# One head's queries first, the log table fetched early, the last pair one by one, and the delta rule's outputs ahead of the third chunk's sums

## The chip, the cores and the metric

The kernel runs on one core of one Trainium2 chip, in one launch. The metric is the device time of the launch in microseconds, the median of three executions: 3196.31 us before the change (3195.89, 3196.31, 3202.15).

## The reference

The input x has 512 tokens of width 1024. 16 meta tokens are put ahead of them, so a first block sees 528. Everything is float32.

```python
# block 1 (attention, then a gated MLP)
h  = concat([meta, x]);  hn = rms_norm(h);  proj = hn @ w_in
o  = concat([sliding_window_attention(...), forgetting_attention(...)])
h  = h + rms_norm(o @ w_out)
h  = h + rms_norm((silu(g) * u) @ w_down)          # [g, u] = rms_norm(h) @ w_gate_up
# block 2
x  = h[16:];  proj = rms_norm(x) @ w_in_2
o_a = rms_norm(gated_delta_rule(q, k, v, beta, g)) * silu(gate_a)    # 8 heads, recurrent over chunks
o_b = rms_norm(hgrn2(q, 1 - f, i, log f)) * sigmoid(gate_b)
x  = x + (sigmoid(g_a) * (o_a @ Wa) + sigmoid(g_b) * (o_b @ Wb)) @ w_out_2
# product keys: 8 heads, 2 x 128 keys a head, 16 of 16384 experts a head and token
h2 = rms_norm(x);  q = h2 @ w_pq                   # 8 heads x 2 halves x 128
s  = q . sub_keys;  top_s, top_i = top_k(s, 16)    # both halves
best, pos = top_k(all 16 x 16 sums, 16);  gate = softmax(best)
y  = sum over the 8 x 16 experts of gate * gelu(h2 . expert_u) * expert_v
return rms_norm(x + y)
```

## The kernel before, in words

Activations lie with their 1024 channels on the partitions (8 tiles of 128 channels by 512 or 528 tokens). All projections are one stream of weight chunks of 512 KB. SyncE loads each into a ring of four. For each chunk ScalarE copies the upper part (`upper`), GpSimd makes the lower part by subtraction (`lower`; in one stage VectorE does), and TensorE multiplies three products for each of 8 channel tiles (`three`): 24 matmuls of 128x512. Two buffers hold upper parts, so `upper(n+2)` waits until chunk n is done. `tile()` on ScalarE is "wait for the next chunk, then start the upper part of the chunk two further on". On ScalarE, GpSimd and TensorE the order is the program's order; nothing overtakes.

**Norms.** TensorE sums squares with a matrix of ones; `inverse_root` on ScalarE makes exp(-0.5 * ln(mean + eps)); VectorE multiplies (`normalise`), ScalarE takes the upper part (`split`), VectorE the lower, and TensorE starts tile by tile. `chunk_root` is the same for a chunk of 128 tokens of the two recurrences. The compiler puts an activation table load ahead of a function that the table held does not have.

**Delta rule.** TensorE, ScalarE and VectorE go through 4 chunks of 128 tokens (c = 0 to 3). In chunk c TensorE makes the state's products (L810, L816), then the sums of squares of chunk c-1 (`sum_chunk`, L801, which waits for the root of chunk c-2), then the state's update (L825) and the chunk's outputs (L831). ScalarE's `outputs` takes the outputs out, in the last chunk also brings back the low part of the next stage's input (`low_part_back`), squares them, and does the root of the chunk before.

**Queries and experts.** The last 16 chunks of the stream are the queries: chunk 2h+half for head h. A part is 2 heads of one tile of 128 tokens, 4 key lists. For a part TensorE makes scores (`key_scores`), VectorE finds the best 16 in five steps (`best_keys_a`, `best_keys_b`, `best_pairs_a`, `_b`, `_c`), ScalarE does the exponential of the gates in between (`gate_exp`), and 32 experts a token are then known (`idx_ready`). GpSimd gathers expert e (one of 512: 4 token tiles by 128) for 128 tokens with an indirect DMA of 1 MB. VectorE takes the dot products of the pair e, e+1 (L2090), ScalarE the gelu of both (L1545), VectorE writes two diagonal matrices (L2098), and TensorE adds diagonal times expert rows to y (two matmuls of 512 columns an expert; L1009 for e below 64 and the rest of the first tile, L1026 and L1036 after).

The first 9 query chunks (`EARLY`) run before the first pair. Scores of part 0 follow the fourth, so VectorE works on part 0 under chunks 4 to 8. The other 7 chunks are cut in halves of 12 matmuls and go ahead of pairs 1, 3, ... 27 (`HALF_AT`); on GpSimd their lower parts sit between the gathers. For e below 64 (the first phase: pairs 0 to 31, `SWITCH`) there are 6 buffers for gathered rows, since the queries' weights still hold the ring; after that 8. Gather e waits until the buffer's last expert has been used by TensorE (`v_used`).

At the end `finish` squares y + x (ScalarE), takes Ln and Exp of the sum, VectorE scales 1024 columns (`scale_out`), and SyncE stores the last 128 tokens.

## Time and profile before

| what | us |
|---|---|
| median of three executions | 3196.31 |
| the profiled execution, device time | 3201.77 |
| its span (first to last instruction) | 3200.0 |
| TensorE busy | 2764.8 (86%) |
| VectorE busy | 1815.2 (57%) |
| GpSimd busy | 1076.4 (34%) |
| ScalarE busy | 865.9 (27%) |
| first gather issued | 1862.12 |

The profile's page cuts the span in 40 slices of 80 us. Busy shares are averages over stages that have different limits: matmul stages up to about 1862 us, gathers after that. The profiled execution took as long as the longest of the three timed ones.

### The profile page before, as it was taken

To read this page: it belongs to the slowest core of one execution; us is meant where nothing else is said; L and a number is where in the kernel's file an instruction comes from. 1 tells how busy PE (TensorE), PEld (TensorE's weight loads), DVE (VectorE), ACT (ScalarE), POOL (GpSimd) and SP (SyncE) were. 2 spreads that over 40 slices of the span, in tenths; PEclk is the share of its full clock that TensorE was granted. 3 is DMA by queue.
4 is the path that set the end of the run, shared out by engine and by line. 5 is a ranking of instruction groups with operands and counts; after the bars stand their busy time and mean duration, and the time that the engine had idled before them with its cause. 6 is when DMAs were issued, how large, how long until landed. Compare 5 with 4: busy or idle time off the path is not lost.

```text
span 3200.0 us, 31098 instructions
## 1 busy us (share of the span) xinstructions
PE 2764.8 (86%) x11130; PEld 1833.4 (57%) x11130; DVE 1815.2 (57%) x3677; ACT 865.9 (27%) x1477; POOL 1076.4 (34%) x722
## 2 busy tenths in 40 slices
PE   7988899998998998999899988887877787777776
PEld 5866578875677976878777654433333333333322
DVE  2056233302576643248833168788777777777765
ACT  3244422223575225233453321100100010001000
POOL 3300234442000002445324345444444444444432
PEclk9999899999998999999999999999899999999999
DMA  4200122222320001221112279999999999999997
GB/s 139 74 14 1 53 86 98 92 99 99 145 73 20 1 27 60 92 92 53 73 66 92 86 297 377 396 421 422 421 412 418 416 409 415 414 410 421 415 422 324
DMA packets 115691, 675.54 MB, mean 211 GB/s; under 512 B 16296, under 2 KB 17768, under 8 KB 49136
## 3 DMA queue, kind: packets, MB, share of 16 engines
q0 software_dynamic: 73728, 536.90, 40.8%
q1 hardware_dynamic: 31536, 114.83, 10.6%
q10 hardware_dynamic: 10304, 22.19, 1.9%
q8 instruction: 74, 1.21, 0.2%
q14 instruction: 49, 0.40, 0.0%
HBM read 667.52 MB, written 6.36 MB: 211 GB/s over the span
## 4 chain that ended last, share of the span: by engine, by line
PE 32%; issue 26%; DMA 21%; DVE 13%; POOL 5%; ACT 3%; ACTq 0%; POOLq 0%; DVEq 0%
DMA arena<-in_experts,arena 21%; PE ps L1036 6%; PE ps L436 6%; PE ps L437 6%; PE ps L438 6%; POOL ring_r L2123 4%; DVE arena L2090 4%; PE ps L1009 3%; DVE arena L2098 1%; DVE arena L1926 1%; PE ps L612 1%; PE ps L584 1%; POOL arena L2158 1%; DVE arena L1925 1%; DVE arena L1908 1%
## 5 line engine op out<-in xcount | busy, mean ns | idle before, releaser
L2123 POOL TENSOR_TENSOR ring_r<-ring,w_hi 128x1024 fp32r<-128x1024 f32 x191 | 470.7, 2465 | 1326.1 <-ACT w_hi L1059 1202.2
L1036 PE MATMUL ps<-arena 128*128 128x512 f32 x1440 | 697.4, 634 | 201.5 <-DVE arena L2098 201.2
L2158 POOL DMA_INDIRECT arena<-in_experts,arena x502 | 553.4, 1102 | 699.4 <-PE ps L1036 485.7
L1036 PEld LDWEIGHTS ps<-arena 128*128 128x128 f32 x1440 | 276.1, 200 | 617.9 <-DVE arena L2098 320.6
L2090 DVE SCALAR_TENSOR_TENSOR arena<-arena,ring 128x1024 f32<-128x1024 f32 x384 | 465.3, 1223 | 182.3 <-DMA arena<-in_experts,arena 180.3
L436 PE MATMUL ps<-n_hi,w_hi 128*128 128x512 f32 (+1 forms) x1264 | 510.9, 404 | 38.2 <-DVE slot_r L1574 14.0
L438 PE MATMUL ps<-n_hi,ring_r 128*128 128x512 f32 (+1 forms) x1264 | 494.6, 391 | 0.0
L1545 ACT ACTIVATE hgel<-hdot 128x2 f32<-128x2 f32 x256 | 52.0, 203 | 1123.9 <-DVE arena L2090 1123.8
L437 PE MATMUL ps<-slot_r,w_hi 128*128 128x512 f32 x896 | 355.4, 397 | 0.0
L1059 ACT ACTIVATE w_hi<-ring 128x1024 fp32r<-128x1024 f32 x175 | 185.1, 1058 | 564.3 <-PE ps L438 556.6
L436 PEld LDWEIGHTS ps<-n_hi,w_hi 128*128 128x128 f32 x1264 | 241.0, 191 | 113.4 <-issue 39.8
L1009 PE MATMUL ps<-arena 128*128 128x512 f32 x472 | 228.0, 630 | 52.8 <-DVE arena L2098 52.7
L438 PEld LDWEIGHTS ps<-n_hi,ring_r 128*128 128x128 f32 x1264 | 241.3, 191 | 54.6
L2098 DVE TENSOR_SCALAR arena<-con,hgel,arena 128x128 f32<-128x128 f32 x512 | 161.5, 403 | 71.5 <-ACT hgel L1545 71.5
L437 PEld LDWEIGHTS ps<-slot_r,w_hi 128*128 128x128 f32 x896 | 170.5, 190 | 42.4 <-issue 6.3
L1009 PEld LDWEIGHTS ps<-arena 128*128 128x128 f32 x472 | 91.3, 200 | 178.5 <-issue 105.2
L437 PE MATMUL ps<-low,w_hi 128*128 128x512 f32 (+1 forms) x496 | 189.5, 382 | 0.0
L2090 DVE SCALAR_TENSOR_TENSOR arena<-arena,gtmp 128x1024 f32<-128x1024 f32 x118 | 150.8, 1294 | 58.3 <-DMA arena<-in_experts,arena 57.9
L1594 DVE SCALAR_TENSOR_TENSOR arena<-arena,par 128x512 f32<-128x512 f32 x16 | 11.7, 744 | 182.5 <-ACT arena L1099 182.5
L437 PEld LDWEIGHTS ps<-low,w_hi 128*128 128x128 f32 x496 | 94.7, 191 | 17.5
L1689 DVE TENSOR_TENSOR arena<-gtmp,ps 128x512 f32 (+1 forms) x22 | 15.1, 687 | 154.5 <-PE ps L438 154.5
L1238 ACT ACTIVATE w_hi<-ring 128x1024 fp32r<-128x1024 f32 x40 | 42.5, 1062 | 170.2 <-PE ps L438 170.2
(336 smaller groups left out, 3963.4 us busy)
## 6 DMA issues: line engine op xcount, KB each, us to landing
ring<-in_weights SPq DMA_DIRECT2D x215, 512.0 KB, 3.5
arena<-in_experts,arena POOLq DMA_INDIRECT x502, 13.0
arena<-decay_rows ACTq DMA_DIRECT2D x2, 2048.0 KB, 11.0
arena<-low_rest ACTq DMA_DIRECT2D x2, 2048.0 KB, 11.0
h_all<-in_xT ACTq DMA_DIRECT2D x2, 1056.0 KB, 6.4
h_rest<-h_all ACTq DMA_DIRECT2D x1, 2048.0 KB, 7.1
low_rest<-slot_r ACTq DMA_DIRECT2D x1, 2048.0 KB, 8.2
h_all<-h_rest ACTq DMA_DIRECT2D x1, 2048.0 KB, 8.6
```

Of the source, the lines that this page charges most:

```text
L436: mm(out, x[0], y[0], start=start, stop=False)
L437: mm(out, x[0], y[1], start=False, stop=False)
L438: return mm(out, x[1], y[0], start=False, stop=stop)
L1009: last = mm(ps[:, half, :], diag[:, at, :], rows_[:, D + half * 512:D + half * 512 + 512], start=e == 0, stop=False)
L1036: last = mm(ps[:, yb + half, :], diag[:, j, :], rows_of[j][:, D + half * 512:D + half * 512 + 512], start=False, stop=False)
L1059: fn(w_hi[:, n % PAIR], ring[:, n % RING], ACT.Copy).then_inc(hi_ready, 1)
L1238: fn(w_hi[:, (c0 + j) % PAIR], ring[:, (c0 + j + 2) % RING], ACT.Copy).then_inc(hi_ready, 1)
L1545: fn(hgel[:, g:g + 2], hdot[:, g:g + 2], ACT.Gelu).then_inc(s["gelu"], 1)
L2090: last = v.scalar_tensor_tensor(rows_[:, 0:D], rows_[:, 0:D], 1.0, h2tok[t], ALU.mult, ALU.mult, accum_out=hdot[:, at:at + 1])
L2098: v.tensor_scalar(diag[:, at, :], ident, hgel[:, at:at + 1], gates[:, t, e % PAIRS:e % PAIRS + 1], ALU.mult, ALU.mult).then_inc(s["diag"], 1)
L2123: g_.tensor_tensor(ring_r[:, n % RING], ring[:, n % RING], w_hi[:, n % PAIR].bitcast(F32), ALU.subtract).then_inc(w_ready, 1)
L2158: g_.indirect_dma_start(rows, None, experts, bass.IndirectOffsetOnAxis(ap=idxu[:, t, col:col + 1], axis=0)).then_inc(landed, 16)
```

## The change

It has five parts.

1. The two query chunks of head 0 are multiplied together, channel tile by channel tile (`first_two_queries`); scores and the best 16 of head 0 alone come next as a piece of their own (piece 0, 2 key lists), head 1 of that part is piece 1, and each later part is one piece (numbered one higher than before).
2. `EARLY` is 5 in place of 9: 11 chunks go in halves ahead of pairs 0, 1, 2, 3, 4, 5, 7, 8, 10, 11, ... 27. Their lower parts on GpSimd follow the gathers of pairs 0, 1, 2, 4, 6, 8, 11 and so on.
3. `fetch_log` is a one-element Ln on ScalarE, put ahead of places where a real Ln comes. At the very start `inverse_root` also moves ahead of `upper(1)`.
4. In the delta rule `sum_chunk(4, 2)` goes behind the last chunk's outputs.
5. The last pair is handled one expert at a time; the residual's last matmuls go ahead of it; the last output tile is scaled and stored in two halves.

```diff
-        EARLY = 9
-        HALF_AT = {2 * h + 1: h for h in range(2 * (16 - EARLY))}
-        SCORES_AT = {13: 2, 29: 3, 40: 4, 50: 5}
+        EARLY = 5
+        CHUNK_AT = [(0, 1), (2, 3), (4, 5), (7, 8), (10, 11), (13, 14), (16, 17), (19, 20), (21, 22), (24, 25), (26, 27)]
+        HALF_AT = {CHUNK_AT[h // 2][h % 2]: h for h in range(2 * (16 - EARLY))}
+        LOWER_AT = {CHUNK_AT[c][1] + 3: EARLY + c + PAIR for c in range(16 - EARLY - PAIR)}
+        SCORES_AT = {6: 2, 18: 3, 28: 4, 40: 5, 50: 6}
-        KEYS_A = {2: 1, 14: 2, 30: 3, 42: 4, 52: 5}
+        KEYS_A = {0: 1, 7: 2, 19: 3, 30: 4, 42: 5, 52: 6}
+        KEYS_B = {1: 1, 8: 2, 21: 3, 32: 4, 44: 5, 54: 6}
+        PAIRS_A = {2: 1, 10: 2, 23: 3, 34: 4, 46: 5, 56: 6}
+        PAIRS_B = {3: 1, 11: 2, 25: 3, 36: 4, 48: 5, 58: 6}
+        PAIRS_C = {4: 1, 12: 2, 27: 3, 38: 4, 50: 5, 60: 6}
+        def piece(p):
+            n = max(0, p - 1)
+            heads = slice(p, p + 1) if p < 2 else slice(0, 2)
+            bank = (6, 5)[p] if p < 2 else 6 + n % 2
+            return n // PARTS, n % PARTS, heads, range(2 * heads.start, 2 * heads.stop), bank
...
@@ TensorE, delta rule
-                    sum_chunk(4, c - 1)
+                    if c < NC - 1:
+                        sum_chunk(4, c - 1)
...
                     last.then_inc(s["os_ready"], 1)
+            sum_chunk(4, NC - 2)
@@ TensorE, queries
+            def first_two_queries():
+                at = count["evac"]
+                count["evac"] += 2
+                pe.wait_ge(evac, at - 1)
+                both = [take(), take()]
+                for k in range(DT):
+                    count["norm"] += 1
+                    pe.wait_ge(norm_ready, count["norm"])
+                    for i, w in enumerate(both):
+                        last = three(ps[:, 2 + (at + i) % 3, :], [p[:, k, :] for p in w],
+                                     [x[:, k, :] for x in (hi2, parts(3))], k == 0, k == DT - 1)
+                        if k == DT - 1:
+                            last.then_inc(chunk_done, 1)
-            for n in range(EARLY):
-                query_half(n, 0)
-                query_half(n, 1)
-                if n == 0:
-                    by_tokens(0, 0)
-                if n == 3:
-                    pe.wait_ge(keys_in, 16)
-                    pe.wait_ge(evac, TILE["pq"] + 4)
-                    key_scores(0)
-            pe.wait_ge(evac, TILE["pq"] + 8)
+            first_two_queries()
+            by_tokens(0, 0)
+            pe.wait_ge(keys_in, 16)
+            pe.wait_ge(evac, TILE["pq"] + 2)
+            key_scores(0)
+            for n in range(2, EARLY):
+                query_half(n, 0)
+                query_half(n, 1)
+            pe.wait_ge(evac, TILE["pq"] + 4)
             key_scores(1)
@@ TensorE, last part
-                with pe.Fori(0, PART // UV - done) as i:
+                end = n == NPARTS - 1
+                with pe.Fori(0, PART // UV - done - end) as i:
...
+                if end:
+                    for half in range(2):
+                        mm(ps[:, yb + half, 3 * P:4 * P], h_all[:, 4 * half + 3, META + t * P:META + (t + 1) * P],
+                           ident, start=False, stop=False)
+                    ...   # the last 8 experts, y_ready with the last one
@@ ScalarE
+            def fetch_log():
+                fn(small[:, 60:61], small[:, 1:2], ACT.Ln)
             act.wait_ge(dve_link, 1)
+            fetch_log()
...
             upper(0)
+            inverse_root(L)
             upper(1)
-            inverse_root(L)
...
+                if n == 7:
+                    fetch_log()            # out1, and the same for down and out2
                 tile()
...
             inverse_root(SEQ)
+            fetch_log()                    # behind the first root of out1 and of down
             squares_of_h()
...
                     fn(normr[:, :, cs], OT[:, :, cs], ACT.Square).then_inc(s["l2_sq"], 1)
+                    fetch_log()            # in outputs, both recurrences, every chunk
                     if c:
                         chunk_root(roots, c - 1)
...
             def finish(t):
+                if t == TT - 1:
+                    fetch_log()
...
+            for n in range(2):
+                act.wait_ge(chunk_done, count["chunk"] + n + 1)
+                take_queries(n)
+            tile()
+            tile()
+            tok_copy(0, 0)
+            gate_exp(0)
+            for n in range(2, EARLY):
...
+                if pair == LAST_PAIR:
+                    for i in range(2):
+                        act.wait_ge(s["dots"], pair + 1 + i)
+                        fn(hgel[:, g + i:g + i + 1], hdot[:, g + i:g + i + 1], ACT.Gelu).then_inc(s["gelu"], 1)
@@ GpSimd
-            lower_all(values_at + 8 + PAIR, queries_at + EARLY)
+            lower_all(values_at + 8 + PAIR, queries_at + 4)
...
-                if e % PART == 0:
-                    pool.wait_ge(s["idx_ready"], e // PART + 1)
+                if e == 0:
+                    pool.wait_ge(s["idx_ready"], 1)
+                elif e == TOPK:
+                    pool.wait_ge(s["idx_ready"], 2)
+                elif e % PART == 0:
+                    pool.wait_ge(s["idx_ready"], e // PART + 2)
...
-                if pair == 2:
-                    lower(queries_at + EARLY, queries_at + EARLY + 1)
-                    lower(queries_at + EARLY + 1, queries_at + EARLY + 2)
-                half = HALF_AT.get(pair - 2, 0)
-                n = queries_at + EARLY + half // 2 + PAIR
-                if half % 2 and n < CHUNKS:
+                n = queries_at + (4 + pair if pair < EARLY + PAIR - 4 else LOWER_AT.get(pair, 16))
+                if n < CHUNKS:
                     lower(n, n + 1)
```

`scale_out(3)` on VectorE and the last store on SyncE go in two halves of 512 columns each, and VectorE's dot, wait for the gelu and diagonal of the last pair are done for one expert and then for the other.

## Rows read from the trace of the kernel before

**Rows 1.** Windows of the gathers' line: window, length, GpSimd busy (gathers), clock, DMA share, GB/s.

```profile
1862.00:2046.00 184.00, 71.47 (x65) 0.96 0.96 379
2100.00:3100.00 1000.00, 435.55 (x395) 0.95 1.01 416
```

**Rows 2.** Waits of TensorE, 1828 to 2056 us: in total, times, longest.

```profile
PE ps L1009 <- DVE arena L2098: 21.9, 12, 6.1
```

**Rows 3.** Timeline of ScalarE at the start: start, duration, instruction, idle before and releaser.

```profile
6.09 1.28 ACT L1127 ACT_TABLE_LOAD   x1 [6.09 <-DMA h_all<-in_xT]
...
17.02 1.06 ACT L1059 ACTIVATE w_hi<-ring 128x1024 fp32r<-128x1024 f32 x1 [1.34 <-DMA ring<-in_weights]
18.09 1.28 ACT L1097 ACT_TABLE_LOAD   x1
```

**Rows 4.** Timelines of TensorE and ScalarE at the norms of out1 and out2.

```profile
372.55 3.00 PE L493 MATMUL ps<-arena,con 128*128 128x512 f32 x6
374.88 1.28 ACT L1097 ACT_TABLE_LOAD   x1
...
391.22 1.28 ACT L1097 ACT_TABLE_LOAD   x1 [1.52 <-PE ps L493]
...
1806.44 1.28 ACT L1097 ACT_TABLE_LOAD   x1 [1.26 <-PE ps L493]
```

**Rows 5.** Timelines of TensorE and ScalarE in the delta rule.

```profile
1210.70 3.56 PE L801 MATMUL ps<-arena,con 128*128 128x512 f32 x4 [3.09 <-ACT arena L1386]
1215.28 0.60 ACT L1394 ACTIVATE h_all<-ps 128x512 f32<-128x512 f32 x1 [4.72 <-PE ps L831]
1226.82 2.61 PE L801 MATMUL ps<-arena,con 128*128 128x512 f32 x4 [3.56 <-ACT arena L1386]
```

**Rows 6.** TensorE, first query chunk (timeline).

```profile
1812.75 0.77 PE L436 MATMUL ps<-n_hi,w_hi 128*128 128x512 f32 x1 [6.39 <-DVE slot_r L1574]
...
1814.60 0.63 PE L437 MATMUL ps<-slot_r,w_hi 128*128 128x512 f32 x1
1815.02 0.63 PE L438 MATMUL ps<-n_hi,ring_r 128*128 128x512 f32 x1
```

**Rows 7.** Groups of TensorE, 1841.4 to 1869.2 us: line, names, shapes, count, busy, mean ns.

```profile
L436 PE MATMUL ps<-n_hi,w_hi 128*128 128x512 f32 x40 | 15.9, 398 | 0.0
```

**Rows 8.** Timelines: scores, VectorE's steps and the first gather; one later step.

```profile
1840.42 1.13 PE L933 MATMUL ps<-arena 128*128 128x128 f32 x8 [0.78 <-ACT arena L1512]
...
1853.67 3.64 DVE L2049 TENSOR_TENSOR arena<-arena 128x256 f32<-128x256 f32 x4
...
1862.12 1.11 POOL L2158 DMA_INDIRECT arena<-in_experts,arena  x1 [0.17 <-issue]
...
2080.18 1.43 DVE L2049 TENSOR_TENSOR arena<-arena 128x256 f32<-128x256 f32 x4
```

**Rows 9.** Timeline of TensorE: pair 0, pair 5 (both experts), pair 28.

```profile
1876.46 5.39 PE L1009 MATMUL ps<-arena 128*128 128x512 f32 x8 [6.10 <-DVE arena L2098]
...
1907.68 1.88 PE L1009 MATMUL ps<-con,arena 128*128 128x512 f32 x4
1909.40 1.02 PE L1009 MATMUL ps<-arena 128*128 128x512 f32 x2
...
2035.90 1.45 PE L1009 MATMUL ps<-arena 128*128 128x512 f32 x3
```

**Rows 10.** Timeline of the end.

```profile
3185.28 1.22 DVE L2090 SCALAR_TENSOR_TENSOR arena<-arena,ring 128x1024 f32<-128x1024 f32 x1 [1.23 <-DMA arena<-in_experts,arena]
...
3187.19 3.70 PE L1036 MATMUL ps<-arena 128*128 128x512 f32 x8 [1.20 <-DVE arena L2098]
...
3192.50 1.28 ACT L1525 ACT_TABLE_LOAD   x1
3193.79 0.29 ACT L1525 ACTIVATE small<-small 128x1 f32<-128x1 f32 x1
...
3196.95 0.33 SPq L404 DMA_DIRECT2D out<-w_hi_f  x1
```

More of the change, by code:

```diff
@@ L1038, in _ @@
                         last.then_inc(s["v_used"], 1)
-                if n % PARTS == PARTS - 1:
+                if end:
+                    for half in range(2):
+                        mm(ps[:, yb + half, 3 * P:4 * P], h_all[:, 4 * half + 3, META + t * P:META + (t + 1) * P],
+                           ident, start=False, stop=False)
+                    for j in range(UV):
+                        pe.wait_ge(s["diag"], TT * PAIRS - UV + j + 1)
+                        for half in range(2):
+                            last = mm(ps[:, yb + half, :], diag[:, j, :], rows_of[j][:, D + half * 512:D + half * 512 + 512],
+                                      start=False, stop=j == UV - 1)
+                        last.then_inc(s["y_ready" if j == UV - 1 else "v_used"], 1)
+                elif n % PARTS == PARTS - 1:
                     residual_end(t)
@@ L1502, in _, with gate_exp @@
             inverse_root(SEQ, rstd2)
-            def gate_exp(n):
-                act.wait_ge(s["gate_in"], n + 1)
-                gt = gates[:, n // PARTS, (n % PARTS) * PART:(n % PARTS + 1) * PART]
+            def gate_exp(p):
+                t, part, heads, lists, bank = piece(p)
+                act.wait_ge(s["gate_in"], p + 1)
+                gt = gates[:, t, part * PART + heads.start * TOPK:part * PART + heads.stop * TOPK]
                 fn(gt, gt, ACT.Exp).then_inc(s["gate_exp"], 1)
@@ L2008, in best_keys_b @@
                     v.max_index(top_i[:, j, 8:16], top_v[:, j, 8:16], rest[:, j, :])
-                for p in range(2):
-                    last = v.tensor_tensor(pair_sum[:, p, :].rearrange("p (i j) -> p i j", j=TOPK),
-                                           top_v[:, 2 * p, :].unsqueeze(2).to_broadcast([P, TOPK, TOPK]),
-                                           top_v[:, 2 * p + 1, :].unsqueeze(1).to_broadcast([P, TOPK, TOPK]), ALU.add)
+                for h in range(heads.start, heads.stop):
+                    last = v.tensor_tensor(pair_sum[:, h, :].rearrange("p (i j) -> p i j", j=TOPK),
+                                           top_v[:, 2 * h, :].unsqueeze(2).to_broadcast([P, TOPK, TOPK]),
+                                           top_v[:, 2 * h + 1, :].unsqueeze(1).to_broadcast([P, TOPK, TOPK]), ALU.add)
@@ new lines, in best_pairs_a @@
+            def best_pairs_a(p):
+                t, part, heads, lists, bank = piece(p)
+                these = range(heads.start, heads.stop)
+                v.tensor_copy(top_f[:, lists.start:lists.stop, :], top_i[:, lists.start:lists.stop, :])
+                link([v.max(best[:, h, 0:8], pair_sum[:, h, :]) for h in these][-1])
+                left = cand.rearrange("p (n k) -> p n k", n=4)
+                for h in these:
+                    v.max_index(pos_u[:, h, 0:8], best[:, h, 0:8], pair_sum[:, h, :])
+                link([v.match_replace(left[:, h, :], best[:, h, 0:8], pair_sum[:, h, :], NEGS) for h in these][-1])
+                link([v.max(best[:, h, 8:16], left[:, h, :]) for h in these][-1])
+                for h in these:
+                    last = v.max_index(pos_u[:, h, 8:16], best[:, h, 8:16], left[:, h, :])
+                v.tensor_tensor(gates_of_piece(p), best[:, heads, :],
+                                best[:, heads, 0:1].to_broadcast([P, len(these), TOPK]), ALU.subtract
@@ L2045, in best_pairs_b @@
                 link(last)
                 for half in range(2):
-                    for p in range(2):
-                        hp = hit[:, half, p * TOPK:(p + 1) * TOPK, :]
-                        last = v.tensor_tensor(hp, hp, top_f[:, 2 * p + half, :].unsqueeze(1).to_broadcast([P, TOPK, TOPK]),
+                    for h in range(heads.start, heads.stop):
+                        hp = hit[:, half, h * TOPK:(h + 1) * TOPK, :]
+                        last = v.tensor_tensor(hp, hp, top_f[:, 2 * h + half, :].unsqueeze(1).to_broadcast([P, TOPK, TOPK]),
```

157 lines of the change are left out of this document (79 added, 78 removed).

## The prediction

> **What bounds the kernel now.** I read the page's slices first (matmul stages to about 1862 us, then gathers), then windows of the gathers, TensorE's waits in the first phase, and timelines wherever the change touches. The reader is to see three regimes.
>
> From 2100 us on, 395 gathers take 1000 us, 2.53 us each, at 416 GB/s with the DMA share at its ceiling [rows 1]. Nothing in the change touches these: this stretch stays as long as it is, and only its start can move. From 1862 to 2046 us 65 gathers take 184 us, 2.83 us each, at 379 GB/s [rows 1]: six buffers, and a loop from "used by TensorE" through gather, landing, dot, gelu and diagonal back to TensorE. TensorE stalls on diagonals for 21.9 us in all, the longest 6.1 us [rows 2], and is otherwise working on pairs and query halves. Before 1862 us TensorE has its matmuls back to back, except at norms and in the recurrences; there a root on ScalarE (load the Ln table, Ln, load the Exp table, Exp) is what it waits for [rows 3 to 5].
>
> So time can come from an earlier first gather less what the first phase gives back, from roots, and from the last few microseconds. Times below are those of the trace before; each part's shift adds to the next.
>
> **Log table, four norms.** At the start a table load of 1.28 us follows the arrival of x, and the Ln load stands behind `upper(1)`, which waited 1.34 us for its weights and took 1.06 [rows 3]. After: the Ln table is loaded before x arrives (6.09). `upper(0)` ends at 15.7, when the sums are there; Ln can run at 15.7 instead of 18.09 + 1.28 = 19.37. That is 3.7 earlier; `upper(1)` now stands in front of the first `split` and takes back about 0.3: **3.4 us**. Bounds: 2.6 (the two loads alone) and 3.7.
>
> At out1 the sums end at 372.55 + 3.00 = 375.55 and the Ln load at 376.16 [rows 4]: TensorE becomes the late one, so only 0.5 of the 1.28 is gained. The second root of out1 waited for the sums and only then loaded [rows 4]: full 1.28. The one-element Ln behind the first root runs while VectorE makes the first tile, free; without that cover it would cost 1.5 once. Down has the same two places: together 2 x (0.5 + 1.3) = **3.6 us**. Out2 has the full case once: **1.3 us** [rows 4].
>
> The row shows a load of 1.28 us. The Trainium skill (ScalarE: Activation LUTs, What ACT_TABLE_LOAD costs) gives the same 1283 ns and adds about 1380 ns of drain for each switch; by that each hidden load would be worth 2.66. By the rows of the start and of out1 the sum takes 1.28.
>
> **Delta rule.** In chunk 3 TensorE waits 3.09 us for the root of chunk 1, makes the sums of chunk 2, and only then the outputs, which ScalarE takes at 1215.28 [rows 5]. With the sums behind, the outputs are ready about 1208, and ScalarE, free of the root of chunk 1 at 1210.6, is the late one. In chunk 1 the Ln table is now there (1.28 less), in later chunks `fetch_log` stands directly ahead of the load and adds its own 0.2 to 0.3 (a one-element Ln is 0.29, [rows 10]). So ScalarE is free at 1210.6 - 1.3 + 0.2 = 1209.5, not 1215.3: 5.8 earlier. Then the low parts come back, the square, the fetch (0.2) and the root of chunk 2, for which TensorE waits with the last sums (3.56 us, ending 1226.82) [rows 5]; that wait stays, all of it earlier. The moved sums need the same root of chunk 1 and run beside the low parts. **5.7 us**; bounds 3.1 (only TensorE's wait) and 6.5. In the second recurrence ScalarE is the late one throughout and the extra Ln costs 2 or 3 x 0.2: **-0.5 us**.
>
> Norms and recurrences: 3.4 + 3.6 + 1.3 + 5.7 - 0.5 = **13.5 us** (8 to 16).
>
> **First queries.** The first query matmul is at 1812.75; matmuls follow each other by 0.42 us at the lower clock (1.2 GHz) [rows 6], until the granted clock, read in windows, is back at its upper level (2.4 GHz) at about 1818.5; then 40 x 3 matmuls take 27.8 us, 0.232 each [rows 7]. Two chunks are 48 matmuls: 13 slow ones to 1818.5, 35 x 0.232 = 8.1, end 1826.6. Two copies out and half as many scores follow: VectorE starts at about 1828.0, not 1841.6 [rows 8]. Its steps took 17.5 us (1841.6 to 1859.1), of which 3.64 - 1.43 = 2.2 were a subtraction on GpSimd holding up a tensor_tensor [rows 8]. Half the lists: 7.7, plus 1.0 for links that don't halve, plus 1.7 of the same hold-up, since `lower` of chunks 2 and 3 now falls there: 10.4, done at 1838.4. The Trainium skill (SBUF — State Buffer, Who interferes with whom) has a VectorE instruction with two SBUF inputs and a GpSimd one that reads SBUF block each other whole; the row agrees with that.
>
> The first gather goes out at 1838.7 instead of 1862.12: 23.4 earlier. It had also waited for GpSimd's subtraction; that is now behind gathers 0 and 1. TensorE has bubbles: chunk 2's lower part is ready only at 1831 (two copies out to 1827.4, an upper part of 1.06, a subtraction of 2.40; 3.1 us idle), chunk 4's at 1843.6, behind two gathers of 1.24 and again 2.40 (1.4 idle). Chunks 2 to 4 end at 1849.2, the first half of chunk 5 at 1852.5. The first diagonal came 13.9 us after the first gather [rows 8, 9], now 1852.6: pair 0 on TensorE at 1852.5 instead of 1876.46, **24.0 us** earlier.
>
> **What the first phase gives back.** A half is 12 x 0.232 = 2.79 us, a pair 2 x 1.72 = 3.44 (1907.68 to 1909.40 for one expert) [rows 9]. Pairs 0 to 5 have a half each: 6.23 us a pair, which is slower than the loop, so pair 5 starts at 1852.5 + 31.2 = 1883.7, still 24.0 ahead of 1907.68. Pairs 5 to 28 took 2035.90 - 1907.68 = 128.2 us for 23 pairs [rows 9]. Floors for these: TensorE before 23 x 3.44 + 11 x 2.79 + 2.6 (scores, residual) = 112.4, DMA before 46 x 2.53 + 2 weight loads of 0.5 MB (1.26 us each at 416 GB/s) = 118.9. So the loop took 9.3 over the higher floor. After: TensorE 79.1 + 16 x 2.79 + 3.7 = 127.4, DMA 116.4 + 6 x 1.26 = 124.0. With the same 9.3 on top: 136.7, pair 28 at 2020.4. Instead of 24.0 that leaves **15.5 us**. Bounds: at best no stall at all, 24.0 + 128.2 - 127.4 = 24.8; at worst every added thing lengthens the loop (rival E). I take the middle, since the loop before, the nearest row there is, kept its distance to the floor.
>
> GpSimd's queue: 12 subtractions between gathers instead of 7, 2.40 us each, but placed one pair later after their upper part than before, so it should not wait for ScalarE. VectorE has half a part more, 7.9 us; pairs 7, 8, 10, 11, 12 now all carry a step, which is its tightest stretch. ScalarE stands in `gate_exp(0)` until VectorE delivers at about 1835, just before chunk 2 ends at 1836.6; if VectorE were later, `upper(4)` would be too. From pair 28 on nothing differs.
>
> **The end.** After the last dot (3185.28 + 1.22) TensorE had four matmul steps for two experts and the residual, 3187.19 to 3191.3; now one expert: 1.72 + 0.26, 2.1 less. The Ln load of 1.28 goes under the last pair. Two halves on VectorE cost about 0.1 more than one pass, the last store carries half the bytes (0.0 to 0.5 less). **3.5 us** (2.5 to 4.2) [rows 10].
>
> **Sum.** 13.5 + 15.5 + 3.5 = 32.5 us. The span goes from 3200.0 to 3167.5, the profiled execution from 3201.77 to 3169.3. That execution is 5.5 above the median; the same 32.5 from 3196.31 gives 3163.8: **3164 us**.
>
> **Rivals.**
>
> A. *TensorE alone sets the first phase.* If landings keep up, pairs 5 to 28 need only 127.4: 24.8 instead of 15.5. For it: the full halves of pairs 0 to 5 let the diagonals get ahead. Against: the loop took 9.3 over its floor before. 3164 - 9 = **3155**.
>
> B. *VectorE's steps bound the loop.* In pairs 7 to 12 VectorE has 6 x 3.4 (two dots of 1.22, a gelu's wait, two diagonals) + 15.4 (one part without the hold-up) = 35.8 us of work and some 3 of hold-ups against 31.8 of TensorE; if the same happens at 19 to 27 and hold-ups with the subtractions add 2, about 8 us more are lost. For it: two steps in adjacent pairs. Against: before, such steps lay in every other pair and the loop came only 9.3 us over its floor. **3172**.
>
> C. *The earlier gathers bring nothing:* subtractions 4, 5 and 6 wedge between the first gathers, TensorE's bubbles grow, and pair 28 is where it was. 3164 + 15.5 = **3180**.
>
> D. *One table less a root.* As a mechanism here: if the load ahead of each Exp went too, six norms' roots and the last one would give 7 x 1.28 = 9.0 more: **3155**. The rows show two loads a root, and the change adds no Exp, so this is unlikely. The Trainium skill (ScalarE: Activation LUTs, Table sets: the hidden batching unit) says that Ln followed by Exp needs one load, since one set has both; the two loads in the trace here say otherwise for this program.
>
> E. *Slower.* In pairs 0 to 31, with six buffers, everything added lies in the loop one behind another: 8 halves x 2.79 = 22.3, 5 subtractions x 2.40 = 12.0, 4 weight loads x 1.26 = 5.0, half a part on VectorE 7.9, together 47.2 against 24.0: 23.2 later, less 13.5 and 3.5: 6 us slower, **3202**. It decides from a pair period of 5.6 + (24.0 + 17.0)/32 = 6.9 us on. Against it: only 21.9 us of TensorE's time in this phase were waits [rows 2], so most of the halves replace work that was done before the first gather.
>
> **How the numbers follow.** Forecast 3164: 0.50 (its own range 3158 to 3169). A 0.16, B 0.17, C 0.08, D 0.03, E 0.04, anything else 0.02. Range 3150 to 3182. Taking 0.2% (6 us) as what a measurement of this kernel can tell: all but E lie beyond it, C and the rest leave something for "same": faster 0.92, same 0.04, slower 0.04.
>
> **What would show it.** Right: first gather about 37 us earlier on the trace's clock (23.4 and the 13.5 before it); pair 0 to pair 28 on TensorE 168 us instead of 159; gather rate unchanged at 2.53 after 2100; no table load ahead of Ln at L1097's places and in the last `finish`; the wait before the moved sums gone. Wrong: pair period above 6.3 us in pairs 5 to 28, waits of GpSimd for `w_hi`, or a stretch after pair 32 that is longer than before.

## The result

The changed kernel takes 3171.22 us (median of four runs, 3167.68 to 3176.65) beside 3196.10 for the kernel before on the same chip (3195.26 to 3202.15): the medians differ by 24.9 us, and the ratio is 0.9918, 95% interval 0.9905 to 0.9932, so 26 us less. Timed twice more, with four runs each beside 11 and 15 of the kernel before, the ratio was 0.9898 (0.9883 to 0.9913) and 0.9909 (0.9894 to 0.9924). The mean of the three is 0.9908, 29 us. The forecast was 32.5 us less, 3164 in a range of 3150 to 3182: the result is right in sign and inside the range, and the forecast was some 3 to 6 us too good (7 us by the median of the first timing).

The profiled execution of the changed kernel is 3172.77 us with a span of 3171.0; that of before was 3201.77 with 3200.0. Between them lie 29.0 us.

First the gathers' own line by windows, columns as in [rows 1], from the first gather to the end of the first phase and in the steady stretch:

```profile
1828.00:2022.00 194.00, 77.79 (x65) 0.98 0.96 373
2100.00:3100.00 1000.00, 446.21 (x395) 0.95 1.01 417
```

The steady stretch is what it was, 395 gathers in 1000 us. The first phase needs 194 us for the 65 gathers that took 184. TensorE's waits in it, 1802 to 2022 us, to be read beside the 21.9 us of [rows 2]:

```profile
PE ps L1038 <- DVE arena L2179: 7.3, 5, 4.1
PE ps L452 <- DVE slot_r L1639: 5.1, 1, 5.1
PE ps L452 <- POOL ring_r L2204: 3.2, 2, 2.6
```

Waits for diagonals are down to 7.3 us, and one of them is 4.1. TensorE's timeline at pair 0, around pair 9, and at pair 28, as in [rows 9]:

```profile
1843.90 2.41 PE L1038 MATMUL ps<-arena 128*128 128x512 f32 x5 [1.69 <-DVE arena L2179]
...
1899.62 6.63 PE L1038 MATMUL ps<-arena 128*128 128x512 f32 x8 [4.12 <-DVE arena L2179]
...
2012.39 1.45 PE L1038 MATMUL ps<-arena 128*128 128x512 f32 x3
```

Pair 0 to pair 28 takes 168.5 us; it was 159.4, and the forecast said 168. Pair 9 waits 4.12 us, since one of its diagonals takes 3.09 us on VectorE and ends 0.1 us behind a subtraction of GpSimd:

```profile
1896.47 3.09 DVE L2179 TENSOR_SCALAR arena<-con,hgel,arena 128x128 f32<-128x128 f32 x1 [0.27 <-ACT hgel L1610]
...
1897.12 2.35 POOL L2204 TENSOR_TENSOR ring_r<-ring,w_hi 128x1024 fp32r<-128x1024 f32 x1
```

The start, VectorE and GpSimd in the moments that decide the first layer-1 matmul, and that matmul:

```profile
4.75 1.28 ACT L1133 ACT_TABLE_LOAD   x1 [4.75 <-issue]
...
15.06 0.68 ACT L1141 ACTIVATE arena<-ps,small 128x528 f32<-128x528 f32 x1
15.76 1.28 ACT L1143 ACT_TABLE_LOAD   x1
...
18.72 2.73 POOL L2204 TENSOR_TENSOR ring_r<-ring,w_hi 128x1024 fp32r<-128x1024 f32 x1 [1.15 <-ACT w_hi L1099]
...
19.28 2.74 DVE L1639 TENSOR_TENSOR low<-arena,n_hi 128x528 fp32r<-128x528 f32 x1
...
18.19 3.57 PE L540 MATMUL ps<-arena,par 33*8 33x512 f32 x4 [4.69 <-DMA con<-in_consts]
...
22.16 0.77 PE L452 MATMUL ps<-n_hi,w_hi 128*128 128x512 f32 x1 [0.41 <-DVE low L1639]
```

ScalarE does what was forecast: the Ln load is over before x arrives, Ln starts at 15.06 instead of 19.37. But the first lower part of x lasts 2.74 us on VectorE, where the second such operation takes about 0.7. GpSimd's subtraction for chunk 1 starts half a microsecond before it; in the profiles without the early start (23.63 us in that of before) the same operation takes 0.71. A second thing stands close behind: four small matmuls for the relative bias (L540) wait for constants and end at 21.76, so that the first layer-1 matmul could not have started earlier than that here.

The delta rule, beside [rows 5]: TensorE's last outputs, the moved sums, and the sums of the last chunk, with ScalarE's copy of the outputs.

```profile
1201.00 1.95 PE L848 MATMUL ps<-arena,vnew 128*128 128x128 f32 x16
1204.34 1.96 PE L817 MATMUL ps<-arena,con 128*128 128x512 f32 x4 [1.39 <-ACT arena L1437]
1215.30 3.01 PE L817 MATMUL ps<-arena,con 128*128 128x512 f32 x4 [2.82 <-ACT arena L1437]
...
1204.11 1.07 ACT L1445 ACTIVATE h_all<-ps 128x512 f32<-128x512 f32 x2
```

The outputs are done at 1202.95 (1201.00 + 1.95) and wait for ScalarE, which takes both at 1204.11 without a pause, where [rows 5] has it idle for 4.72 us. The sums wait 1.39 us beside ScalarE's other work, and nothing queues behind them but the projection. The last rows are the first query chunk and the first gather, then the end. TensorE's wait ahead of the first query matmul was 6.39 us in [rows 6] and is 5.12, one table load less:

```profile
1802.10 0.77 PE L452 MATMUL ps<-n_hi,w_hi 128*128 128x512 f32 x1 [5.12 <-DVE slot_r L1639]
...
1828.29 1.11 POOL L2243 DMA_INDIRECT arena<-in_experts,arena  x1 [6.46 <-DVE arena L2136]
...
3159.95 1.23 DVE L2171 SCALAR_TENSOR_TENSOR arena<-arena,ring 128x1024 f32<-128x1024 f32 x1 [0.55 <-DMA arena<-in_experts,arena]
...
3161.44 1.28 ACT L1133 ACT_TABLE_LOAD   x1
...
3165.26 0.29 ACT L1582 ACTIVATE small<-small 128x1 f32<-128x1 f32 x1
```

The first gather is 26.2 us behind the first query matmul, against 49.4 in [rows 6, 8]. On the traces' clock it comes 33.8 us earlier, and 39.6 and 37.9 us earlier in two more profiles of the changed kernel; the forecast said about 37. At the end the Ln load lies at 3161.44, under TensorE's last pair, and Ln follows the square at once.

### The profile page after: what moved, and what is told of

Read it like the earlier page. It is cut to its first block, busy times and chain, and to the rows that moved or that the text cites. A ratio compares the mean times of both kernels' runs of the same rounds, so it can differ in the third digit from the quotient of the medians.

```text
span 3171.0 us, 31129 instructions
## 1 busy us (share of the span) xinstructions
PE 2767.2 (87%) x11130; PEld 1838.0 (58%) x11130; DVE 1826.8 (58%) x3708; ACT 869.3 (27%) x1495; POOL 1093.2 (34%) x722
## 4 chain that ended last, share of the span: by engine, by line
PE 38%; issue 21%; DMA 19%; DVE 14%; POOL 3%; ACT 3%; PEld 1%; ACTq 0%; PEldq 0%; POOLq 0%; DVEq 0%
DMA arena<-in_experts,arena 19%; PE ps L452 8%; PE ps L453 8%; PE ps L454 8%; PE ps L1066 6%; DVE arena L2171 4%; PE ps L1038 3%; POOL ring_r L2204 2%; DVE arena L2179 1%; PE ps L628 1%; DVE arena L1991 1%; POOL arena L2243 1%; PE ps L600 1%; DVE arena L1990 1%; DVE arena L1973 1%
## 5 line engine op out<-in xcount | busy, mean ns | idle before, releaser
L1066 PE MATMUL ps<-arena 128*128 128x512 f32 x1408 | 682.4, 634 | 196.1 <-DVE arena L2179 195.5
L2243 POOL DMA_INDIRECT arena<-in_experts,arena x502 | 565.4, 1126 | 691.4 <-PE ps L1066 475.0
L1066 PEld LDWEIGHTS ps<-arena 128*128 128x128 f32 x1408 | 270.3, 200 | 603.4 <-DVE arena L2179 312.4
L1038 PE MATMUL ps<-arena 128*128 128x512 f32 x472 | 224.6, 621 | 45.6 <-DVE arena L2179 45.6
L1038 PEld LDWEIGHTS ps<-arena 128*128 128x128 f32 x472 | 90.1, 197 | 166.8 <-issue 95.5
L2171 DVE SCALAR_TENSOR_TENSOR arena<-arena,gtmp 128x1024 f32<-128x1024 f32 x118 | 144.4, 1243 | 46.0 <-DMA arena<-in_experts,arena 45.3
```

Source lines behind the costliest of these rows:

```text
L1038: last = mm(ps[:, half, :], diag[:, at, :], rows_[:, D + half * 512:D + half * 512 + 512], start=e == 0, stop=False)
L1066: last = mm(ps[:, yb + half, :], diag[:, j, :], rows_of[j][:, D + half * 512:D + half * 512 + 512], start=False, stop=False)
L2171: last = v.scalar_tensor_tensor(rows_[:, 0:D], rows_[:, 0:D], 1.0, h2tok[t], ALU.mult, ALU.mult, accum_out=hdot[:, at:at + 1])
L2243: g_.indirect_dma_start(rows, None, experts, bass.IndirectOffsetOnAxis(ap=idxu[:, t, col:col + 1], axis=0)).then_inc(landed, 16)
```

## The experiments

Times carry noise from one execution to the next: the kernel before ran from 3195.3 to 3208.0 us over all comparisons. So every experiment was timed against the kernel before on its own chip, and its profile was cut at fixed points of TensorE's work. The points are the starts of the n-th pass, that is, of the n-th call of `three` on TensorE counted from 0, the first gather, pairs 0 and 28, and the last gather. Pass 328 is the first behind the norm of out1 and pass 856 the first behind that of down. The delta rule lies between passes 1008 and 1056, the second recurrence between 1368 and 1504. Each length comes from one profiled execution.

**Early Ln loads and the start alone.**

```diff
+            fetch_log()            # also ahead of other roots
...
             upper(0)
+            inverse_root(L)
             upper(1)
-            inverse_root(L)
```

> The kernel before with the early Ln fetches and the reordered start alone. The prediction's terms: start 3.4 + first norms 3.6 + out2 1.3, less 0.5 in the second recurrence = 7.8 us, so 3188.4 by the median of 3196.2. Rival, from the traces of before and after: these places gave about 2.3 (start), 3 (norms) and nothing further, and the second recurrence took 3: some 3 to 5 us, 3192. The place to read: distance of the first query chunk from the first layer-1 matmul, and the second recurrence's stretch.

Measured 0.9972 (0.9964 to 0.9981), 9 us less: the forecast's 7.8 is inside the interval of 6 to 11.5. The first layer-1 matmul starts at 22.21 us against 24.2 to 24.6 in the five profiles that lack this edit. The delta rule's stage is only 0.4 us shorter (289.7 us against 290.1 in the kernels with the query part or the end alone), where the forecast had 1.3 for the loads there.

**The moved sums alone**, twice.

```diff
-                    sum_chunk(4, c - 1)
+                    if c < NC - 1:
+                        sum_chunk(4, c - 1)
...
+            sum_chunk(4, NC - 2)
```

> The kernel before with the third chunk's sums moved behind the delta rule's last outputs, and nothing else. Predicted for this move together with the early fetches there: 5.7 us; of that 1.3 were two Ln fetches, so 4.4 here. Traces of before and after give 6.4 for the stretch from the inverse to the last sums. Theory: 4 to 6 us, 3191. Rival (the sums are only put off, the final root waits for them all the same): under 1 us, 3195.5.

Measured 1.0000 (0.9991 to 1.0008): nothing. Yet its profile is 4.1 us shorter over the delta rule and the stages before it (from pass 1008 to pass 1056: 286.0 us, against 290.1 in two kernels that have neither this edit nor the early loads; the first profile of the kernel before has 287.1, for a reason given below), and the second recurrence (pass 1368 to 1504) is 4.0 us longer. So I ran it again.

> The move of the delta rule's sums alone, a second time. From the start of the 1008th weight pass to the 1056th (the delta rule and what is before it) its first profile was 4.1 us shorter than the kernels with the query part or the end alone, and the second recurrence 4.0 us longer, by an extra low-clock stretch. Theory A (the stretch belongs to this kernel: its work reaches the second recurrence at another place): the recurrence is at 155 us again and the ratio at 1.000. Theory B (it falls there in some executions of any kernel, as it did in one of two profiles of the changed kernel): 151.5 us, the ratio between 0.9985 and 1.

Measured 0.9998 (0.9988 to 1.0007). The second recurrence is again 4 us longer. The next rows give one window on TensorE over it, of the kernel with the end alone (this stage as before), then of the first and the second profile of the moved sums; columns: window, length, busy (count), granted clock, DMA share, GB/s.

```profile
1470.31:1621.71 151.40, 132.13 (x1036) 0.97 0.17 60
```

```profile
1466.42:1621.79 155.37, 137.01 (x1036) 0.92 0.17 58
```

```profile
1468.38:1623.72 155.34, 136.98 (x1035) 0.92 0.17 58
```

The same instructions, the same DMA, and 4 us more at a mean clock of 0.92 instead of 0.97. Theory A held as far as two profiles can tell: the stretches at the low level (1.2 GHz) recur in this kernel. What the sums gain is given back 250 us later, in a stage whose code is untouched. TensorE's waits there are nearly the same in both kernels: 1.7, 4.1, 4.7, 1.9, 1.9 and 1.6 us, each to 0.1. But behind the first two the low stretch lasts 10.2 us in the second profile of the moved sums and 6.8 in the kernel with the end alone, and behind the last three 13.7 against 3.4. Two later waits shrink in return (1.7 to 0.6 and 1.6 to 1.1 us). Why the clock stays low longer when the same work comes 2 to 4 us earlier is not settled.

**The query part alone.**

```diff
-        EARLY = 9
+        EARLY = 5
...
-            for n in range(EARLY):
+            first_two_queries()
+            by_tokens(0, 0)
```

> The kernel before with the query part alone (two chunks first, one head's selection, first gather early, chunks respread). Predicted 15.5 us; the traces of before and after give 12.8 for pair 0 to pair 28 and what is before it. Theory A: part of the shortfall is a hold-up of pair 9's two diagonals by GpSimd's subtraction, which recurs in this kernel as it follows from the order of work: 13 us, 3183, with the pair 9 diagonals at over 2 us again. Rival: that hold-up was an accident of the one execution: it is absent in this profile, and the gain is 17 to 19 us, 3178.

Measured 0.9957 (0.9944 to 0.9970), 13.8 us, where the forecast had 15.5. From the first query matmul to the first gather 26.75 us instead of 49.4; pair 0 to 28 took 169.95. The hold-up recurred: one of pair 9's two diagonals took 2.96 us, though TensorE waited longest at pair 12 (4.4 us). VectorE at pair 9 in this profile:

```profile
1905.43 3.22 DVE L2137 TENSOR_SCALAR arena<-con,hgel,arena 128x128 f32<-128x128 f32 x2 [0.27 <-ACT hgel L1575]
```

**The end alone.**

```diff
-                fn(hgel[:, g:g + 2], hdot[:, g:g + 2], ACT.Gelu)...
+                if pair == LAST_PAIR:
+                    for i in range(2):
+                        act.wait_ge(s["dots"], pair + 1 + i)
```

> The kernel before with the last pair taken one expert at a time, the last store in two halves and the Ln of the last norm fetched early. Predicted 3.5 us, traces of before and after give 3.7: 3192.6. Rival (the last landing bounds the end whatever follows it): under 1 us.

Measured 0.9995 (0.9986 to 1.0004): by times alone unclear. The trace decides for the stage: from the last gather to the end of the span 24.76 us, against 28.38 to 28.60 in five profiles without it. The four parts alone sum to 24 us (9.0 + 0.0 + 13.8 + 1.6), the three timings of the whole give 26 to 33.

**The changed kernel again**, and once more later.

> The changed kernel unchanged, for more times and a second profile. By the sum of its four parts run alone (9.0 + 0.0 + 13.8 + 1.6 us) the ratio to the kernel before is 0.9924, by the first timing 0.9918. In the trace, what the order of work fixes recurs (pair 9's diagonals over 2 us, late outputs of the delta rule gone); the places of the low-clock stretches away from TensorE's long waits need not.

> The changed kernel unchanged, as the measure for the two kernels built on it, and a third profile. Ratio to the kernel before 0.990 to 0.992; pair 28 168 us behind pair 0; second recurrence at 151.5 or 154.4 us.

Ratios 0.9898 and 0.9909. Pair 0 to 28: 168.09 and 169.17. The second recurrence took 151.47 and 151.44 us, but 154.45 in the first profile. Here is its window there, and the same in the third:

```profile
1460.33:1614.78 154.45, 134.63 (x1036) 0.96 0.17 59
```

```profile
1459.00:1610.44 151.44, 131.63 (x1036) 0.98 0.17 60
```

**The changed kernel without the moved sums.**

```diff
-                    if c < NC - 1:
-                        sum_chunk(4, c - 1)
+                    sum_chunk(4, c - 1)
...
-            sum_chunk(4, NC - 2)
```

> The changed kernel with the delta rule's third sums back in their old place. Theory A (the move is worth nothing to the end, since what it gains before the 10th stage is given back by an extra low-clock stretch in the second recurrence, as in the kernel with the move alone): within 0.1% of the changed kernel. Theory B (the move is worth its 4 to 6 us once the other edits stand beside it): 3 to 6 us slower than the changed kernel.

Measured 0.9914 (0.9902 to 0.9927) beside 0.9898 (0.9883 to 0.9913) for the changed kernel on the same chip: 5 us by the ratios, but the intervals overlap, so the times don't decide. The trace does for the stage: 289.8 us from pass 1008 to 1056 with the other edits in, 284.1 in all three profiles of the changed kernel. The move carries 5.7 us there, against 4.1 alone, and in the profile without it the second recurrence takes 151.6 us, no less than in two of the changed kernel's three: nothing is given back there.

**Subtractions in quarters.** GpSimd's subtraction of a query chunk in pairs 0 to 31 as four instructions.

```diff
+                for k in range(0, DT, 2):
+                    part = g_.tensor_tensor(ring_r[:, n % RING, k:k + 2], ring[:, n % RING, k:k + 2],
+                                            w_hi[:, n % PAIR, k:k + 2].bitcast(F32), ALU.subtract)
```

> The changed kernel with each of GpSimd's subtractions of a query chunk in the first 32 pairs issued as four of a quarter each. Theory A (a VectorE operation on the diagonals has to wait until the running GpSimd subtraction ends, 2.4 us): diagonals of no pair take over 1.3 us, pair 9's wait of 4.1 us on TensorE shrinks, and the phase gives back 1 to 3 us less. Theory B (the two share the port over time, whatever the size of the instructions): diagonals as slow as before, no gain.

VectorE's diagonals, 1835 to 2045 us, in the changed kernel's second profile and with quarters (shortest, median and longest of one, in ns, then the first and last start):

```profile
L2179 DVE TENSOR_SCALAR arena<-con,hgel,arena x72: 334/346/3092, 1836.4 to 2043.7; 128x128 f32<-128x128 f32 x72
```

```profile
L2179 DVE TENSOR_SCALAR arena<-con,hgel,arena x70: 334/382/855, 1845.8 to 2044.7; 128x128 f32<-128x128 f32 x70
```

Theory A held: the longest falls from 3.09 to 0.86 us. TensorE's wait at pair 9 is 1.95 us instead of 4.12. But the hold-ups are partly spread and not gone: VectorE's dots become slower (1324 ns in the mean instead of 1245), and TensorE waits 1.94 us at pair 12. The phase takes 166.8 us, 1.3 less than the shortest of three. The time as a whole, 0.9908 (0.9890 to 0.9926), does not resolve 1.3 us.

**Matmuls without use in TensorE's waits.** Their results are read by nobody.

```diff
+            def warm(times):
+                for _ in range(4 * times):
+                    mm(ps[:, 7, 0:P], ones, ones, start=True, stop=True)
```

> The changed kernel plus matmuls without use (ones times ones, 128 columns, into bank 7) in TensorE's long waits: 32 ahead of each sum over h, 28, 32 and 28 behind the meetings 4, 6 and 18, 40 behind meeting 7. In the changed kernel low-clock stretches of 6.8 to 10.2 us lie behind these waits (at 376, 390, 772, 789, 967 and 1800 us: 44 us). Theory A (the stretches are brought on by TensorE's idle time just before them): they go, and the kernel is up to 44/2 = 22 us faster, 12 to 20 with what waits for other engines; about 3156. Theory B (they come for another reason, or the time is bound elsewhere there): within 2 us of the changed kernel. Rival C: the extra matmuls hold up what they stand before: slower by up to 6 us.

Measured 0.9915 (0.9902 to 0.9928), 5 us slower than the changed kernel beside it by the ratios. Each takes about 0.23 us, so they overran the waits. Behind meeting 7 they stood in full after the wait instead of in it. That is rival C. Next they were fitted in number, and in place at meeting 7:

> The changed kernel with matmuls without use in TensorE's long waits, now as many as fit by their measured 0.228 us: 22 ahead of each sum over h, 20, 23 and 20 behind the meetings 4, 6 and 18, and 28 between drain and wait of meeting 7. In the first such kernel they overran the waits by 1.4 to 1.9 us each and by 8.7 us at meeting 7, and the stretches behind them were gone. Theory: without the overrun what the clock gives back remains, 1.5 to 3 us at each of six places: 8 to 14 us faster than the changed kernel. Rival: what follows those waits is bound by other engines, under 3 us.

Measured 0.9904 (0.9889 to 0.9919) beside 0.9909 for the changed kernel: no gain that the runs can tell. TensorE by windows around the norms of out1 and down, meeting 7 and the first queries (columns as above), first the changed kernel's third profile, then the fitted one:

```profile
370.00:400.00 30.00, 18.84 (x42) 0.77 0.02 9
768.00:800.00 32.00, 19.92 (x45) 0.79 0.25 97
966.00:1010.00 44.00, 34.58 (x247) 0.81 0.01 3
1796.00:1816.00 20.00, 14.85 (x61) 0.90 0.14 52
```

```profile
370.00:400.00 30.00, 26.84 (x125) 1.00 0.06 18
768.00:800.00 32.00, 28.51 (x134) 1.00 0.22 83
966.00:1010.00 44.00, 38.51 (x299) 0.92 0.04 13
1796.00:1816.00 20.00, 19.58 (x105) 1.00 0.24 84
```

The clock did what the theory said: 0.77 to 1.00, 0.79 to 1.00. The time did not. From pass 328 to 856, which holds the whole norm of down, and from 856 to 864, the fitted kernel takes 398.88 and 16.17 us, the changed one 398.89 and 16.17. The reason stands in TensorE's timeline at the first chunk behind the norm, in the fitted kernel:

```profile
393.40 0.47 PE L452 MATMUL ps<-n_hi,w_hi 128*128 128x512 f32 x1 [0.28 <-DVE low L1649]
...
394.57 0.51 PE L452 MATMUL ps<-n_hi,w_hi 128*128 128x512 f32 x1 [0.23 <-DVE low L1649]
```

At full clock TensorE waits for each tile of VectorE's normalisation. At the low clock, in the changed kernel, it has no such waits behind the first tile: a tile's three matmuls take 1.28 us there, about as long as VectorE needs for the next tile. Only behind meeting 7 and at the first query chunks, where no other engine paces the matmuls, did the clock pay: 5.2 us less from pass 1008 to 1056 and 1.5 less from the first query matmul to the first gather. And 4.0 of these went again in the second recurrence (155.5 us instead of 151.4), 2.4 more from pass 864 to 1008 (128.2 instead of 125.8). The kernel with quarters, whose code there is that of the changed kernel, also takes 128.1, so the 2.4 are scatter.

**Fitted matmuls and quarters together**, also for chunks 0 and 1 at the start.

> The kernel with the fitted matmuls, and GpSimd's subtractions in quarters for chunks 0 and 1 and for the query chunks of the first 32 pairs. By the profile of the kernel with quarters in the pairs (pair 0 to pair 28 in 166.8 instead of 168.1 to 168.6 us) 1.3 to 1.7 us less there, and the first layer-1 matmul up to 1 us earlier, if chunk 1's subtraction (2.73 us at 18.72) is what held VectorE's 2.74 us operation. Together 2 to 3 us below the fitted kernel. Rival: nothing, the phase takes back what the start gives.

Measured 0.9894 (0.9879 to 0.9909), the lowest ratio of all, 34 us below the kernel before; its interval overlaps that of the changed kernel (0.9894 to 0.9924), and the changed kernel had 0.9898 on another chip, so that it beats it is not shown. What the profile shows is the start, here with GpSimd's chunk 1, VectorE's first lower part, and TensorE:

```profile
18.81 4.58 POOL L2221 TENSOR_TENSOR ring_r<-ring,w_hi 128x256 fp32r<-128x256 f32 x4 [0.71 <-ACT w_hi L1109]
...
19.37 1.12 DVE L1649 TENSOR_TENSOR low<-arena,n_hi 128x528 fp32r<-128x528 f32 x1
...
18.12 2.48 PE L545 MATMUL ps<-arena,par 33*8 33x512 f32 x4 [4.05 <-DMA con<-in_consts]
20.63 0.77 PE L452 MATMUL ps<-n_hi,w_hi 128*128 128x512 f32 x1
...
22.85 0.79 PE L452 MATMUL ps<-n_hi,w_hi 128*128 128x512 f32 x1 [0.60 <-DVE low L1649]
...
27.36 0.65 PE L452 MATMUL ps<-n_hi,w_hi 128*128 128x512 f32 x1
```

VectorE's operation takes 1.12 us instead of 2.74, and the first matmul starts at 20.63 instead of 21.97 to 22.51. GpSimd pays: four quarters take 4.58 us where one piece took 2.73.

But nothing of it is left four passes later. Pass 4, the last row above, starts at 27.36 us, in the first profile of the changed kernel at 27.42. VectorE's next three operations take 1.23 us each where 0.7 to 0.8 is usual, so its hold-up is spread over four operations. Part of the early first matmul is also the clock: the matmuls for the bias (L545) end at 20.60 instead of 21.76, as the low stretch began at 19.3 instead of 18.0 us.

## Why the prediction was right, and where it missed

The table has lengths between fixed points of TensorE's work in us. "Before" and "after" are the two first traces; "all" compares the median of the profiles that lack the edits of a stretch with that of the changed kernel's three.

| stretch | forecast | before to after | all |
|---|---|---|---|
| start to first layer-1 matmul | -3.4 | -2.3 | -2.2 |
| start to pass 1008 (norms of out1, down) | -3.6 | -5.8 | -2.7 |
| pass 1008 to 1056 (delta rule) | -5.7 | -3.0 | -6.0 |
| pass 1056 to 1504 (second recurrence) | +0.5 | +2.5 | -0.5 |
| pass 1504 to first query (out2) | -1.3 | -2.1 | -1.3 |
| first query to first gather | -23.4 | -23.2 | -23.7 |
| first gather to pair 0 | -0.6 | +1.3 | +1.2 |
| pair 0 to pair 28 | +8.5 | +9.1 | +9.1 |
| pair 28 to last gather | 0 | -1.9 | -0.7 |
| last gather to end | -3.5 | -3.6 | -3.6 |
| sum | -32.5 | -29.0 | -30.4 |

*First queries and first gather.* Right to 0.3 us, and by the steps that the forecast gave: VectorE starts 14.9 us behind the first query matmul (15.3 forecast) and needs 11.1 us for one head's best 16 (10.4 forecast), of which about 2.0 are a tensor_tensor of 2.34 us beside GpSimd's subtraction (1.7 forecast).

*What the first phase gives back.* The number is right to 0.6 us, but partly by luck. Pairs 0 to 5 took 31.2 us, 6.24 us a pair, as forecast. For pairs 5 to 28 the forecast took the higher floor (TensorE's, 127.4) plus the same 9.3 as before. Measured are 137.3 us (136.9 and 138.0 in the other two profiles), 9.9 over that floor. TensorE in that stretch, in the first traces of before and after:

```profile
1907.68:2035.90 128.22, 117.27 (x346) 0.99 0.97 381
1875.12:2012.39 137.27, 132.27 (x421) 0.98 0.95 368
```

Before, the 9.3 were the distance to the floor of the DMA (118.9). Over TensorE's own floor of 112.4 the loop took 15.8: TensorE was busy for 117.3, which is 4.9 more than counted, and waited 10.9. After, it is busy for 132.3, again 4.9 more than counted, and waits only 5.0. So no distance was kept. After, the 9.9 are 4.9 of work that the count left out and 5.0 of waits; before, the waits alone were 10.9.

Most of the excess lies in one place. Pairs 7 to 12 take 39.8 us, 8.0 over TensorE's counted 31.8 (39.3 to 39.8 in three profiles). Here is VectorE in them, before and after:

```profile
1917.34:1953.30 35.96, 26.69 (x53) 0.95 1.00 397
1885.68:1925.43 39.75, 36.94 (x101) 0.91 0.89 344
```

VectorE is busy for 93% of these pairs, where it was 74% before, and TensorE's wait of 4.1 us at pair 9 is there, with a low-clock stretch of 6.8 us right behind it. That is rival B's mechanism, at about the size that B gave it (35.8 us of VectorE's work and some 3 of hold-ups). It did not recur in pairs 19 to 27, and it stands in place of the forecast's 9.3 and not on top of them. B's 3172, though it is close to the measured median, was not reached by the whole of B's way. In this term the forecast had the right size and B, for pairs 7 to 12, the right cause. Rivals A (24.8 of gain kept) and C (nothing kept) are out. Rival E's point, a pair period of 6.9 us, was not reached in the mean: it is 5.97 us over pairs 5 to 28, though pair 9 alone took 9.3.

*Delta rule.* 5.7 forecast, 6.0 found. The two parts are not additive: the early loads give 0.4 alone and 1.9 beside the move (286.0 to 284.1), the move 4.1 alone and 5.7 beside the loads. Why is not settled. The rival that the sums are merely put off is refuted by the stage's length. Before to after shows only 3.0, as the first trace of before happened to lack the low-clock stretch near 1151 us that two other profiles with the same code there have: it took 287.1 us, they 290.1.

*Start.* This term was mis-sized: 3.4 forecast, 2.2 found. The step "Ln can run 3.7 earlier, `upper(1)` takes back 0.3" held on ScalarE, where Ln came even 4.3 earlier. It failed one engine on: VectorE's first subtraction came to lie beside GpSimd's for chunk 1 and lost 2.0 us. I had priced just this collision in the selection and did not ask for it at the start. The quarters bring the first matmul forward by 1.3 to 1.9 us, but pass 4 hardly at all (27.36 beside 27.42 to 27.61), so they do not show that the loss can be had back. What the collision itself costs stays open, as in the first profile the bias matmuls hold the first layer-1 matmul until 21.76 anyway.

*Norms.* 3.6 forecast for out1 and down, and cut close to them 3.6 found: 40.4 to 38.7 us from pass 320 to 336, and 47.4 to 45.5 from 848 to 864 (medians of five profiles without and three with the edit). The 2.7 of the table holds 0.9 of scatter in the first layer, where nothing was changed. For out2 the wait ahead of the first query matmul fell by 1.27 us.

*First gather to pair 0.* Forecast 0.6 faster, found 1.2 slower. The second dot of pair 0 takes 2.01 us where 1.22 is usual, and its two diagonals 1.92 where 0.6 is. Beside them stand GpSimd subtractions that I had counted on TensorE's side only. That they cause this loss is argued and not shown: in the kernel with quarters in the pairs the stretch takes 15.4 us, where the changed kernel has 15.5 to 15.6. The timeline of both engines in the changed kernel:

```profile
1835.44 2.78 POOL L2204 TENSOR_TENSOR ring_r<-ring,w_hi 128x1024 fp32r<-128x1024 f32 x1
...
1837.30 2.01 DVE L2171 SCALAR_TENSOR_TENSOR arena<-arena,gtmp 128x1024 f32<-128x1024 f32 x1 [1.32 <-DMA arena<-in_experts,arena]
...
1841.38 2.37 POOL L2204 TENSOR_TENSOR ring_r<-ring,w_hi 128x1024 fp32r<-128x1024 f32 x1
...
1842.18 1.92 DVE L2179 TENSOR_SCALAR arena<-con,hgel,arena 128x128 f32<-128x128 f32 x2 [2.87 <-ACT hgel L1610]
```

*The rest.* The 3.1 us in the second recurrence of the first trace of after are low clock; two other profiles of the same kernel don't have them. The forecast's 32.5 less the two misses (1.2 and 1.8) is 29.5 us, and the mean of three timings is 29. This agreement is loose, since single stages scatter by 3 to 4 us.

On the rules weighed in the forecast. Each hidden table load gained at most its 1.28 us: the norms of out1 and down 1.7 and 1.9 for two places each, out2 1.3. The 2.66 a load that the Trainium skill (ScalarE: Activation LUTs, What ACT_TABLE_LOAD costs) gives with the drain is not seen. Rival D is out too: every root still loads a table for Exp, at 15.76 and 3165.57 among others. The rule of the Trainium skill (SBUF — State Buffer, Who interferes with whom) that the two engines block each other whole agrees with the runs: the diagonals that met a whole subtraction ended 0.1 us behind it, at pair 9 after 3.09 us, and beside quarters none took more than 0.86.

## What to carry to other kernels

When a step is moved by a few microseconds, list what every engine that shares a resource is doing at the new time, at every place and not only where the change is large; at both misses here a VectorE operation landed beside a GpSimd one. Making the GpSimd operation short lowers the worst hold-up (3.1 to 0.9 us with quarters, 1.3 us of the phase), but where VectorE works without a pause it only spreads it, as at the start. When a floor plus a distance gives the right number, look what fills the distance before using it again: here it was waits before, and one overloaded stretch of VectorE after. Cut each trace at fixed points of the work and compare stage lengths over several profiles. Many stages repeat to 0.1 us, others jump by 3 to 4 when a low-clock stretch falls in them, and a single pair of traces can show half or twice a term.

## What the runs showed of the hardware

- A gain of 4.1 us in one stage came back as a loss of 4.0 in an untouched one, in both of two profiles, with the same instructions and DMA at a mean clock of 0.92 instead of 0.97, and the times agree (1.0000 and 0.9998).
- Raising the clock from 0.79 to 1.00 around the norm of down moved nothing (398.88 and 398.89 us), since VectorE paced TensorE there. It paid where no other engine did: 5.2 us behind meeting 7.
- A 128-column matmul of f32 operands takes 0.23 us at the upper clock: 22 of them, which the fitted kernel's trace lists as 44 entries, took 5.08 us.
- Beside VectorE at work, GpSimd's subtraction in four pieces took 4.58 us against 2.73 in one, and VectorE's was 1.12 against 2.74: dividing the instruction shifted waiting from one engine to the other, and TensorE's pass 4 came at the same time (27.36 and 27.42).
